# A transformer layer on one core: x, the embeddings and the norm vectors turned by the layout of the inputs instead of by TensorE

## The reference, cut to what matters

```python
def rmsnorm(x, g):
    return x * rsqrt(mean(x * x, -1) + EPS) * g

u = rmsnorm(x, mix_norm_g)
q, k, v = split(u @ wqkv)                 # q and k get a norm per head, with a_q_norm_g and a_k_norm_g
h = x + banded_softmax(q, k, v, alibi, sinks) @ wo
h = h + square(relu(rmsnorm(h, mlp_norm_g) @ w1)) @ w2
h = h + sigmoid(rmsnorm(h, ple_norm_g) @ w_gate) * (p @ w_proj)
```

## Time and profile before

| | |
|---|---|
| median of 3 runs | 1082.61 us (1081.87 to 1082.89) |
| profiled execution: span from its first to its last instruction | 1080.2 us |
| TensorE busy in it | 1066.7 us, 99% |
| VectorE, ScalarE, GpSimd busy | 72%, 44%, 14% |
| attention, from the loop's first scores | about 30 to 240 us |
| output projection, MLP | about 240 to 972 us |
| gate and embeddings | about 972 us to the end |

### The profile page before, as it was taken

The page is one execution under the profiler, slowest core; times in us unless marked ns, Lnnn a source line. Parts: engine busy times, 40 slices in busy tenths (PEclk is TensorE's granted clock), DMA queues, the critical chain, the costliest instruction groups (busy, mean ns, idle before and its releaser), DMA issues.

```text
span 1080.2 us, 14531 instructions
## 1 busy us (share of the span) xinstructions
PE 1066.7 (99%) x5014; PEld 884.2 (82%) x5014; DVE 779.9 (72%) x1147; ACT 478.0 (44%) x841; POOL 149.6 (14%) x271
## 2 busy tenths in 40 slices
PE   8999999999999999999999999999999999999998
PEld 6788888887888888888888888888888888888887
DVE  7877877778344599776677668376776878747985
ACT  7566676667323233413322342353333335427451
POOL 7644544443000000000000000000000000001000
PEclk9999999999999999999999999999999999999999
DMA  7000000050332325353343254998888898660102
GB/s 273 21 21 19 19 19 26 14 195 20 117 118 78 117 75 203 131 196 122 149 178 150 84 194 177 389 413 281 289 284 290 294 327 315 212 234 1 39 30 88
DMA packets 67232, 167.49 MB, mean 155 GB/s; under 512 B 5088, under 2 KB 6376, under 8 KB 67176
## 3 DMA queue, kind: packets, MB, share of 16 engines
q1 hardware_dynamic: 67152, 166.75, 42.8%
q10 hardware_dynamic: 24, 0.01, 0.0%
HBM read 128.99 MB, written 37.75 MB: 154 GB/s over the span
## 4 chain that ended last, share of the span: by engine, by line
PE 88%; DVE 7%; issue 2%; ACT 1%; POOL 1%; DMA 1%; SPq 0%; ACTq 0%; POOLq 0%; DVEq 0%
PE pair L2565 28%; PE pair L2545 22%; PE pair L2269 10%; PE pair L2413 8%; PE pair L2611 6%; PE pair L2503 3%; PE pair L2340 3%; PE pair L2308 2%; PE pair L2638 2%; PE pair L2252 1%; PE pair L2473 1%; PE pair L2319 1%; DMA RES<-in_a_wqkv 1%; PE pair L2234 0%; POOL k_rstd L790 0%
## 5 line engine op out<-in xcount | busy, mean ns | idle before, releaser
L2565 PE MATMUL pair<-uT 128*128 128x512 f32 x1344 | 305.9, 389 | 0.0
L2565 PEld LDWEIGHTS pair<-uT 128*128 128x128 f32 x1344 | 252.0, 188 | 52.5 <-DVE uT L1957 0.3
L1296 ACT ACTIVATE uT<-wo_raw 128x1024 fp32r<-128x1024 f32 x83 | 84.6, 1054 | 113.5 <-PE pair L2565 97.3
L1957 DVE TENSOR_TENSOR uT<-wo_raw,uT 128x1024 fp32r<-128x1024 f32 x83 | 98.6, 1222 | 45.6 <-ACT uT L1296 45.1
L772 POOL TENSOR_SCALAR row_var<-row_ssq 128x1 f32<-128x1 f32 x16 | 3.1, 197 | 708.6 <-ACT hn L1337 625.5
L2413 PE MATMUL pair<-WA,oT 128*128 128x512 f32 x384 | 90.3, 392 | 0.6 <-DVE oT L1720 0.4
L2269 PE MATMUL pair<-WA,xT 128*128 128x512 f32 x336 | 83.9, 398 | 1.2 <-DVE xT L1516 0.4
L2413 PEld LDWEIGHTS pair<-WA,oT 128*128 128x128 f32 x384 | 71.2, 188 | 16.0 <-issue 1.4
L2545 PE MATMUL pair<-WA,WB 128*128 128x512 f32 x336 | 78.2, 389 | 0.4 <-ACT xr L1271 0.4
L2545 PEld LDWEIGHTS pair<-WA,WB 128*128 128x128 f32 x336 | 63.0, 188 | 13.8 <-DVE WB L1891 0.8
L2269 PEld LDWEIGHTS pair<-WA,xT 128*128 128x128 f32 x336 | 60.9, 188 | 14.6 <-issue 2.3
(11 more groups left out here) (239 smaller groups left out, 1790.4 us busy)
## 6 DMA issues: line engine op xcount, KB each, us to landing
wo_raw<-in_m_w SPq DMA_DIRECT2D x71, 512.0 KB, 6.4
wo_raw<-hid_kept SPq DMA_DIRECT2D x41, 512.0 KB, 5.9
hid_kept<-RES SPq DMA_DIRECT2D x32, 512.0 KB, 2.7
emb<-in_m_w SPq DMA_DIRECT2D x17, 512.0 KB, 5.7
RES<-in_m_w SPq DMA_DIRECT2D x8, 1024.0 KB, 6.7
uT_f<-in_m_w SPq DMA_DIRECT2D x6, 1024.0 KB, 6.7
RES<-in_a_wqkv SPq DMA_DIRECT2D x10, 512.0 KB, 8.6
emb<-hid_kept SPq DMA_DIRECT2D x10, 512.0 KB, 5.7
```

What stands on the lines that cost most here:

```text
L1296: nc.scalar.activation(operand(t, which, HI), unit(t, which), ACT.Copy).then_inc(op_hi, 1)
L1957: nc.vector.tensor_tensor(operand(t, which, LO), unit(t, which), operand(t, which, HI).bitcast(F32), ALU.subtract).then_inc(op_ready, 1)
L2565: mm = nc.tensor.matmul(ps[4 * (j % 2) + m][:], operand(t, 0, s)[:, k, m * P:(m + 1) * P], operand(t, 1, r)[:, k, :], start=(g == 0 and k ...
```

## The change

The host hands over x, the embeddings p and the norm vectors in two layouts: x as before, and x turned (`x_turned`, per partition the eight tiles of a block side by side), p turned (`p_turned`), and the norm vectors as ten columns (`head_cols`). A load brings each block of turned x into a buffer `xt`; the parts of xT are made from there, in whole rows of 1024 except for the first block, which comes in two halves. x itself is still loaded, for its squares; its first load now stands behind four weight units. The parts of the embeddings are made from their buffer, in two rows of 1024 each in place of four of 512. The turnings of x, of the embeddings and of the vectors on TensorE go, with the waits that they needed.

```diff
-            sp.dma_start(xb[:], x[0:P, :]).then_inc(x_in, 16)
+            for hf in range(2):
+                sp.dma_start(xt[:, 4 * hf:4 * hf + 4, :], x_turned[:, 0, 4 * hf:4 * hf + 4, :]).then_inc(xt_first[hf], 16)
             for u in range(U_W1):
+                if u == 4:
+                    sp.dma_start(xb[:], x[0:P, :]).then_inc(x_in, 16)
...
             def load_x(b):
 
-                sp.wait_ge(xT_done, 2 * b)
+                sp.wait_ge(xT_ready, b + 1)
+                sp.dma_start(xt[:], x_turned[:, bass.ds(b, 1)].rearrange("p b k n -> p (b k) n")).then_inc(xt_in, 16)
                 sp.wait_ge(x_squared, b)
                 sp.dma_start(xb[:], x[bass.ds(b * P, P), :]).then_inc(x_in, 16)
...
-            sp.dma_start(emb[:], p.rearrange("(b p) n -> p b n", p=P)).then_inc(emb_in, 16)
+            sp.dma_start(emb[:].rearrange("p b n -> p (b n)").rearrange("p (k n) -> p k n", k=PT),
+                         p_turned).then_inc(emb_in, 16)
...
-            def xT_hi_half(b, hf):
-                act.wait_ge(xT_done, 2 * b + (1 + hf))
-
-                wait(act, projected["q8"], b)
-                nc.scalar.activation(xT[:, HI, 4 * hf:4 * hf + 4, :], x_bank(b, hf)[:].rearrange("p (k n) -> p k n", k=4),
+            def xT_hi_part(b):
+                act.wait_ge(xt_in, 16 * b)
+                act.wait_ge(projected["q8"], b)
+                nc.scalar.activation(xT[:, HI], xt[:], ACT.Copy).then_inc(xT_hi, 1)
...
-            act.wait_ge(gain_zero, 1)
-            act.dma_start(gain[0:KT, 0:P], mix_g.rearrange("(k p) -> k p", p=P)).then_inc(gain_in, 16)
-            for row, g in ((0, gq), (1, gk)):
-                act.dma_start(gain[row:row + 1, P:2 * P].rearrange("a (r d) -> a r d", r=2),
-                              g.partition_broadcast(2).unsqueeze(0)).then_inc(heads_in, 16)
-
+            act.dma_start(columns[:], head_cols).then_inc(columns_in, 16)
...
             def keep_p1(m):
                 act.wait_ge(gate_done, tile_done("P1", m))
-                act.wait_ge(emb_turned, 4)
+                act.wait_ge(eT_ready, PT)
...
-            def xT_lo_half(b, hf):
-                dve.wait_ge(xT_hi, 2 * b + (1 + hf))
-                nc.vector.tensor_tensor(xT[:, LO, 4 * hf:4 * hf + 4, :], x_bank(b, hf)[:].rearrange("p (k n) -> p k n", k=4),
+            def xT_lo_part(b):
+                dve.wait_ge(xT_hi, b + 2)
+                nc.vector.tensor_tensor(xT[:, LO], xt[:], xT[:, HI].bitcast(F32), ALU.subtract).then_inc(xT_ready, 1)
...
             def project(X, b, kts=range(KT)):
 
-                pe.wait_ge(xT_ready, 2 * b + 2)
+                pe.wait_ge(xT_ready, b + 2)
+                if X == "q0":
+
+                    pe.wait_ge(T_ready["q0"], 2 * b)
...
-                    if j == 0 and not last:
-                        if first:
-                            project("q0", 1, kts=range(0, 2))
-                        else:
-                            turn_x(n + 1)
+                    if j == 0 and first:
+                        project("q0", 1, kts=range(0, 2))
...
-            warm_up(WARM_UP // 3)
-            turn_small(0)
-            turn_x(0)
-            warm_up(WARM_UP // 3)
-            project_first("k", (HI, 0))
-            turn_small(1)
-            project_first("k", (HI, 1), (LO, 0), (HI, 2), (LO, 1), (HI, 3), (LO, 2), (LO, 3))
+            warm_up(2 * WARM_UP // 3)
+            project_first("k", (HI, 0), (HI, 1), (LO, 0), (HI, 2), (LO, 1), (HI, 3), (LO, 2), (LO, 3))
...
             gate("P1", 0)
-            turn_emb(0)
-            turn_emb(1)
             gate("P1", 1)
             turn_d(4)
-            turn_emb(2)
-            turn_emb(3)
             gate("P1", 2)
...
+            "x_turned": x.reshape(blocks, P, tiles, P).transpose(3, 0, 2, 1),
+            "p_turned": p.reshape(p.shape[0], p.shape[1] // P, P).transpose(2, 1, 0),
```

More of the change, by code:

```diff
@@ L59, with trunk_layer @@
 SPILLED = ("z11", "z22", "m1", "m2", "m5", "m6", "m7")
-def trunk_layer(nc, x, p, mix_g, mlp_g, ple_g, wqkv, gq, gk, sinks, wo, w1, w2, w_proj, w_gate, out):
+def trunk_layer(nc, x, x_turned, p_turned, head_cols, mlp_g, ple_g, wqkv, sinks, wo, w1, w2, w_proj, w_gate, out):
     T, D = x.shape
-    HD = gq.shape[0]
     H = sinks.shape[0]
+    HD = wo.shape[0] // H
     QKV = wqkv.shape[1]
@@ L72, in trunk_layer @@
     MT = BANK // P
-    PT = p.shape[1] // P
+    PT = p_turned.shape[1]
     NC = D // BANK
@@ L377, in trunk_layer @@
         pT_bank = (ps[4], ps[5])
-        tr_bank = (ps[6], ps[1])
-        def x_bank(b, hf):
-            return ps[7] if isinstance(b, int) and (b, hf) == (1, 1) else tr_bank[hf]
         consts_in = sem("consts_in")
@@ L408, in trunk_layer @@
         x_eps = sem("x_eps")
[L409 to L413, removed]
+        columns_in = sem("columns_in")
+        gq_ready = sem("gq_ready")
+        xt_first = [sem(f"xt_first{i}") for i in range(2)]
+        xt_in = sem("xt_in")
         xT_hi = sem("xT_hi")
@@ L1448, in _ @@
             eT_hi_part(0)
-            eT_hi_part(1)
             proj_unit(0)
@@ L2222, in _ @@
         def _(pe):
-            def turn_x(b):
-                pe.wait_ge(ident_ready, 2)
-                pe.wait_ge(x_in, 16 * (b + 1))
-                wait(pe, T_ready["k"], b)
-                if not (isinstance(b, int) and b == 1):
-                    wait(pe, T_ready["q0"], 2 * b)
-                for hf in range(2):
-                    for k in range(4):
-                        kt = 4 * hf + k
-                        mm = nc.tensor.transpose(x_bank(b, hf)[:, k * P:(k + 1) * P], xb[:, kt * P:(kt + 1) * P], ident[:])
-                    mm.then_inc(xT_done, 1)
             def project_first(X, *parts):
@@ L2363, in body @@
                             project("q0", n + 1, kts=range(2 if first else 0, 5))
-                        turn_q("q8", n, after_x=not last)
+                        turn_q("q8", n)
                         if not last:
@@ L2696 @@
     shape = inputs["x"].shape
+    x = np.asarray(inputs["x"]).reshape(shape[-2:])
+    p = np.asarray(inputs["p"]).reshape(np.asarray(inputs["p"]).shape[-2:])
+    blocks, tiles = x.shape[0] // P, x.shape[1] // P
+    laid = {"x": x,
+            "x_turned": x.reshape(blocks, P, tiles, P).transpose(3, 0, 2, 1),
+            "p_turned": p.reshape(p.shape[0], p.shape[1] // P, P).transpose(2, 1, 0),
+            "head_cols": np.concatenate([np.asarray(inputs["mix_norm_g"]).reshape(tiles, P).T]
+                                        + [np.tile(np.asarray(inputs[g]).reshape(-1), 2)[:, None]
+                                           for g in ("a_q_norm_g", "a_k_norm_g")], axis=1)}
+    for name in _INS:
+        a = np.asarray(inputs[name])
+        laid[name] = a.reshape(a.shape[1:])
     nc = bacc.Bacc("TRN2", target_bir_lowering=False, num_devices=1, dynamic_dma_scratch_size=1024)
     arrays, args = {}, []
-    for name in _INS:
-        a = np.ascontiguousarray(inputs[name])
-        a = a.reshape(a.shape[2:] if name == "p" else a.shape[1:])
+    for name, a in laid.items():
+        a = np.ascontiguousarray(a)
         arrays[f"in_{name}"] = a
```

102 lines of the change are left out of this document (37 added, 65 removed).

## The result

The changed kernel takes 1085.04 us (median of 7 runs, 1084.55 to 1086.46), the kernel before 1081.89 us in the same session (7 runs, 1081.36 to 1082.89). The ratio is 1.0029, 95% interval 1.0018 to 1.0039: slower by about 3.1 us. The profiled spans, 1083.3 and 1080.2 us, differ by as much, so the two traces can be laid side by side. Each line of this table is a moment that both traces have; the fourth column is what the stretch since the line above added.

What follows compares the result with a forecast made beforehand. TensorE, 99% busy, was taken to be held next by VectorE in the loop and by loads in the opening. 1.19 + 0.37 - 0.72 - 0.80 = +0.04 us gave 1082.6 us; range 1079.3 to 1086.1.

Steps and rivals of the forecast that it cites:

- the rival about VectorE and GpSimd in the loop: Attention loop: xT's low part waits for GpSimd's q_rstd, +2.76 us over six iterations, 1086.1 in all; chance 0.08.
- the prediction's signs of being wrong: Loop period falling by 0.5 us or more, period growing, or ScalarE finding its fifth weight unit already landed.
- The start: Opening: 512 KB put ahead of the fifth weight unit make the first scores 1.19 us later; bounds 0 to 1.75.
- so I cost that at nothing: Opening: one more load issue on SP ahead of the second weight unit costs nothing, 0.47 us if wrong.
- does not belong to TensorE: First 32 us: the timeline was read as an opening that TensorE does not set.
- Block 1: First loop iteration: whole rows in place of halves make VectorE's next work 0.37 us later; bounds 0.2 and 0.5.
- The loop: Blocks 2 to 7: without the transposes, xT's low part on VectorE limits the gain to 0.12 us an iteration, 0.72 for six.
- The hand-off of 0.06 us: Loop: time from the end of xT's low part at 92.39 to TensorE's start of q0's projection at 92.45.
- The embeddings: Sixteen transposes go in two sets; only the first set's removal counts, a gain of 0.80 us; bounds 0.4 and 1.6.
- that chain is 4.78 us long with or without the second set: Embeddings: fifth to sixth transposing of h, over ScalarE, GpSimd and VectorE, stays 4.78 us, so the second set gives nothing.
- TensorE as the bound: Rival: each loop iteration gives back 0.87 us and both embedding sets count, 1077.3 us; chance 0.17, half of it included.
- the reordered loads cost nothing: Rival in the opening: the fifth weight unit lands when it did before, sum -1.15, 1081.4 us; no separate chance given.

Runs made afterwards that it cites:

- the two loop experiments: Changed kernel with VectorE's loop order turned: 1084.51 us, ratio 1.0027; the same plus the q8 heads' transposes one projection step later: span 1082.5.

## Why the prediction was wrong

The forecast was no change, and the kernel became slower by more than a measurement can miss; the measured time lies inside the range, near its upper end, by luck: that end was set by the rival about VectorE and GpSimd in the loop, which did not come true there. None of the prediction's signs of being wrong came either: the period neither fell by 0.5 us nor grew by more than 0.05, and ScalarE did wait 1.21 us for its fifth unit. Three of the four terms came out beyond the bounds given for them, all in the same direction; of the cases named, the one nearest to it had 0.06, a start that costs more than its bounds.

*The start, +1.19 forecast, +2.24 measured.* The 512 KB ahead of the fifth unit were right: from the second unit's landing to the fifth's it is 5.11 us instead of 3.84, 1.27 more (forecast 1.28), and moving them took that wait away. The step that failed is the sentence ahead of it: one more issue, "so I cost that at nothing". With the first load split, every unit from the second on landed 0.69 us later, above the 0.47 allowed, and one load instead of two brought every unit forward by 1.15. The second failure is a term that was not there at all: that the opening "does not belong to TensorE" was read off rows in which TensorE had work almost throughout. The change took out of the opening the transposes that kept it so, and put no work into the gap that the later weights made. The fifth unit accounts for 1.96 us of the 2.24; the other 0.28 is the wait for k's projection at the low clock.

*Block 1, +0.37 forecast, +0.50 measured*, the mechanism as described, and halves gave 0.34 back. (The prediction's own terms, 30.37 and 1.22, make 31.59 and not 31.54, so +0.42.) Another 0.25 us, up to the scores of group 2, was not foreseen; it has a place on VectorE, shown above, but no cause.

*The loop, -0.72 forecast, +0.08 measured.* That VectorE would take over from the transposes was right, and the whole row took the 1.22 us of the earlier trace rows. Counted from the squares of q8, xT's low part ended 0.09 us earlier than before (4.17 instead of 4.26), q0's projection began 0.06 earlier, and its first 15 matmuls gave 0.07 back. The steps that failed are two. The hand-off of 0.06 us was taken from another pair of rows: it is 0.13 to 0.14 in five of the six iterations, and in the earlier trace rows this very wait has 0.11 (92.46 to 92.57), with which the gain would have been 0.07. And the projection behind the wait was taken to be as fast as before: its first matmul is followed by the second after 0.33 us in the changed kernel, 0.27 before. No further wait held TensorE up to the q8 heads in the changed kernel; that other chains stand within half a microsecond behind is what the two loop experiments show, in which the projection began 0.51 us earlier.

*The embeddings, -0.80 forecast, -0.10 measured.* The first half came (0.92). The step that failed is "that chain is 4.78 us long with or without the second set": it was taken to be free of the rest of VectorE's work. The fifth transposing came 0.92 us earlier, T1 on VectorE 0.11 (37.35 us behind the table's fifth moment, 37.46 before), and so `row_var` fell into T1.

*The rivals.* TensorE as the bound is out: the period did not fall. That the reordered loads cost nothing is out as well: the fifth unit landed 1.96 us later. The one about VectorE and GpSimd named the right pair of engines, but in the wrong place and with the wrong one waiting: in the loop xT's low part took its 1.22 us though `q_rstd` ran for its first 0.59 us, and it was GpSimd that was held, `probs<-sink` for 0.72 us instead of 0.20, which delayed nothing. The Trainium skill (SBUF — State Buffer, section "SBUF: two separate sides") gives the port to whichever started first, a VectorE instruction with two SBUF inputs or a GpSimd one that reads SBUF, for its whole instruction. `row_var`, held until 0.06 us after T1's end and back at 0.19 us when T1 was moved, agrees with that; xT's low part beside `q_rstd` does not show it.

## What to carry to other kernels

Work taken off an engine that is 99% busy is worth only the distance to the next wait; ask at once what ends second, and what behind it ends third, because in a loop tuned by hand several chains end within half a microsecond of each other. In an opening that goes at the pace of its loads, count loads as well as bytes, put what is needed late behind what is needed early, and keep TensorE at work up to its first real product. When an engine's work moves in time, look at what the other engines will be doing at its new place.

## What was not expected of the hardware

- Two first loads of 256 KB in place of one of 512 KB put the weight unit that followed back by 0.75 to 1.9 us (it landed at 6.92 to 7.99 in ten runs, at 6.06 to 6.17 in three with one load), more than the 0.47 or 0.62 us of the issue. The reason is open.
- A load of 5 KB, issued on ScalarE's queue behind four weight units on SP's, took 6.7 us, and 1.6 to 4.3 us when it was issued first (3.0 in the changed kernel).
- TensorE's granted clock fell to 0.50 in the ten profiles in which it sat idle for 1.9 us or more ahead of the first weights, and stayed at 1.00 in the four in which the wait was 1.22 us or less. It fell at different times (from 7.8 to 10.6 us) and for different lengths. By the mean clock of executions that were not profiled, it does not fall every time with the same kernel.
- GpSimd instructions of 0.19 to 0.27 us took 0.72 to 0.99 beside a VectorE subtraction or product of two SBUF operands (`row_var`, `probs<-sink` and `q_var` above), while VectorE's xT row took its usual 1.22 us beside `q_rstd`.
